# A weight ring of six units in place of four, the low part in the memory of the raw part, stage loops written out

## What is computed

```python
for i in range(DEPTH):
    kind, j = i % N_MIXERS, i // N_MIXERS
    if kind == 0:
        mix = fox_mixer(h, fox_w_in[j], fox_b_f[j], fox_w_o[j])
    elif kind == 1:
        mix = swa_mixer(h, swa_w_in[j], swa_sinks[j], swa_w_o[j], cos_p, sin_p)
    else:
        mix = mla_mixer(h, mla_w_a[j], mla_g_q[j], mla_g_kv[j], mla_w_uq[j], mla_w_ukv[j], mla_w_o[j],
                        cos_m, sin_m)
    h = layer_norm(DEEPNORM_ALPHA * h + mix, ln1_g[i], ln1_b[i])
    ffn = conv_glu_ffn(h, ffn_w_in[i], ffn_conv_w[i], ffn_conv_b[i], ffn_w_out[i], valid)
    h = layer_norm(DEEPNORM_ALPHA * h + ffn, ln2_g[i], ln2_b[i])
```

## Time and profile before

| | |
|---|---|
| median of 3 runs | 1333.57 us (1332.96 to 1334.44) |
| the profiled execution, own time | 1333.88 us |
| its span, first to last instruction | 1332.1 us |
| granted PE clock, mean | 0.995 of full |
| PE busy | 1296.4 us (97%) |
| DVE, ACT, POOL busy | 938.3, 793.8, 225.8 us |
| weights moved | 377 DMAs of 512 KB |

### The profile page before, as it was taken

How to read it: one execution, slowest core, us unless ns; L and a number is a source line. 1 busy time by engine, 2 the same in 40 slices (tenths; PEclk the granted TensorE clock), 3 DMA queues, 4 the chain that set the end, 5 groups by cost and what they waited for, 6 DMA issues and landing times.

```text
span 1332.1 us, 29945 instructions
## 1 busy us (share of the span) xinstructions
PE 1296.4 (97%) x10381; PEld 1252.5 (94%) x10381; DVE 938.3 (70%) x1877; ACT 793.8 (60%) x1625; POOL 225.8 (17%) x208
## 2 busy tenths in 40 slices
PE   7999999999998999999998999999999999999997
PEld 7999999999887999999987899999999899999997
DVE  4765877765787877765678687776567667777665
ACT  4565666654565676664476667666446565766643
POOL 1000044420000034330001003433000000244300
PEclk9999999999999999999998999999999999999999
DMA  7432465556421455556442045555645334465562
GB/s 267 140 110 80 143 189 185 178 180 198 133 91 49 130 185 184 180 155 213 155 127 80 33 143 187 187 172 165 208 139 158 111 112 127 144 187 189 174 218 83
DMA packets 56723, 202.80 MB, mean 152 GB/s; under 512 B 6208, under 2 KB 8256, under 8 KB 56512
## 3 DMA queue, kind: packets, MB, share of 16 engines
q1 hardware_dynamic: 56640, 201.68, 47.4%
HBM read 200.61 MB, written 1.05 MB: 151 GB/s over the span
## 4 chain that ended last, share of the span: by engine, by line
PE 82%; DVE 7%; ACT 5%; issue 3%; DMA 1%; POOL 1%; ACTq 0%; DVEq 0%; POOLq 0%; SPq 0%
PE ps L385 23%; PE ps L389 22%; PE ps L388 22%; PE ps L535 2%; PE ps L553 2%; ACT probs L889 2%; DVE w_lo L1260 1%; PE ps L424 1%; PE ps L518 1%; PE ps L430 1%; PE ps L427 1%; ACT w_hi L839 1%; DMA raw<-in_weights 1%; POOL gated L1234 1%; DVE scores L1320 1%
## 5 line engine op out<-in xcount | busy, mean ns | idle before, releaser
L1260 DVE TENSOR_TENSOR w_lo<-raw,w_hi 128x1024 fp32r<-128x1024 f32 x377 | 461.1, 1225 | 230.3 <-ACT w_hi L839 228.9
L385 PE MATMUL ps<-h_hi,w_hi 128*128 128x272 f32 (+1 forms) x1752 | 508.6, 290 | 1.8 <-DVE q_rope L1526 1.0
L389 PE MATMUL ps<-h_hi,w_lo 128*128 128x272 f32 (+1 forms) x1752 | 505.8, 289 | 0.0
L388 PE MATMUL ps<-h_lo,w_hi 128*128 128x272 f32 (+1 forms) x1752 | 499.6, 285 | 0.0
L839 ACT ACTIVATE w_hi<-raw 128x1024 fp32r<-128x1024 f32 x377 | 395.0, 1050 | 147.7 <-PE ps L385 136.9
L385 PEld LDWEIGHTS ps<-h_hi,w_hi 128*128 128x128 f32 x1752 | 329.1, 188 | 8.4 <-issue 5.4
L388 PEld LDWEIGHTS ps<-h_lo,w_hi 128*128 128x128 f32 x1752 | 330.0, 188 | 0.3
L389 PEld LDWEIGHTS ps<-h_hi,w_lo 128*128 128x128 f32 x1752 | 328.9, 188 | 0.0
L385 PE MATMUL ps<-hid_hi,w_hi 128*128 128x272 f32 (+2 forms) x636 | 185.4, 292 | 2.2 <-DVE w_lo L1260 1.9
L388 PE MATMUL ps<-hid_lo,w_hi 128*128 128x272 f32 (+2 forms) x636 | 183.1, 288 | 0.0
L389 PE MATMUL ps<-hid_hi,w_lo 128*128 128x272 f32 (+2 forms) x636 | 183.0, 288 | 0.0
(11 more groups left out here) (184 smaller groups left out, 1727.3 us busy)
## 6 DMA issues: line engine op xcount, KB each, us to landing
raw<-in_weights SPq DMA_DIRECT2D x377, 512.0 KB, 3.7
cst<-in_consts SPq DMA_DIRECT2D x1, 1795.5 KB, 12.1
h<-in_x SPq DMA_DIRECT2D x2, 544.0 KB, 5.8
out<-h SPq DMA_DIRECT2D x8, 128.0 KB, 1.7
```

The lines of the kernel that those rows point to most:

```text
L385: m = pe.matmul(b, whi, xhi, start=n == 0, stop=False)
L388: pe.matmul(b, whi, xlo, start=False, stop=False)
L389: m = pe.matmul(b, wlo, xhi, start=False, stop=n == len(tiles) - 1)
L1260: return dve.tensor_tensor(out_, a_, b_, op)
```

## The change

The ring has six units instead of four, so `AHEAD` is five instead of three. The total memory stays as it is (twelve buffers of 4 KB a partition): `raw[s]` and `w_lo[s]` now are the same memory, and `split_lo` writes the low part over the raw weights that it reads. A slot therefore comes free for the next DMA only when PE has used its low part, and SP waits for `w_used` instead of `lo_ready`. `turns` writes its turns out instead of looping. SP's own loop stays. The rest of the diff computes the slot from the unit's absolute number.

```diff
-RING = 4
+RING = 6
 ...
-        raw = [sb(f"raw{s}", [P, UNIT]) for s in range(RING)]
+        with ExitStack() as shared:
+            raw = [shared.enter_context(nc.sbuf_tensor(f"raw{s}", [P, UNIT], F32)) for s in range(RING)]
+        w_lo = [sb(f"w_lo{s}", [P, UNIT], F32R) for s in range(RING)]
         w_hi = [sb(f"w_hi{s}", [P, UNIT], F32R) for s in range(RING)]
-        w_lo = [sb(f"w_lo{s}", [P, UNIT], F32R) for s in range(RING)]
 ...
         def turns(eng, n, emit, first=0):
 
-            if n - first == 1:
-                emit(first)
-            elif n > first:
-                with eng.Fori(first, n) as i:
-                    emit(i)
+            for i in range(first, n):
+                emit(i)
 ...
             def unit(u, s):
 
-                sp.wait_ge(lo_ready, u - (RING - 1))
+                sp.wait_ge(w_used, u - (RING - 1))
 ...
-                    slot = (u0 + u) % RING
+                    slot = un % RING
 ...
-                    split_lo(i * s.body_units + first, first % RING)
+                    split_lo(i * s.body_units + first, (i * s.body_units + first) % RING)
```

More of the change, by code:

```diff
@@ L846, in units_of @@
                         continue
-                    yield (i * s.body_units + first, first % RING,
-                           i * (s.body_units // RING) + (first // RING + 1)
-                           if s.turns > 1 else first // RING + 1)
+                    u = i * s.body_units + first
+                    yield u, u % RING, u // RING + 1
             def gemm(layer, name, evac=None, links=0, straight=False):
@@ L1287, in turn @@
                             for u in s.new_units(j)[:-1]:
-                                if i * s.body_units + u0 + u + AHEAD < N_UNITS:
-                                    split_lo(i * s.body_units + u0 + u + AHEAD, (u0 + u + AHEAD) % RING)
+                                coming = i * s.body_units + u0 + u + AHEAD
+                                if coming < N_UNITS:
+                                    split_lo(coming, coming % RING)
                             late()
```

## The result

The changed kernel takes 1470.57 us (median of 4 runs, 1466.75 to 1474.78) against 1333.26 us (4 runs): a ratio of 1.1031 with a 95% interval of 1.0998 to 1.1064. The forecast was 1468. The profiled execution spans 1464.6 us, 132.5 more than before, at a mean clock of 0.957 against 0.995. It is the execution whose own time is 1466.75 us, the fastest of the four.

The account below looks back on a forecast made before the run. PE, busy 1296.4 of 1332.1 us, was taken as the bound, so new waits ahead of it count in full. Stalls of 101.6 us plus 33 us of clock made 134.6 us on 1333.88: 1468 us, range 1425 to 1502.

Parts of the forecast that it names:

- fox pairs: Stages `qk` of two fox layers: scores start 3.03 us later per pair, 7.5 stalls a layer, 45.4 us.
- LayerNorm tails: Ends of `o` and `down`: squares and sums queue behind late splits, 4 x 3.5 + 3 x 3.8 = 25.4 us.
- starts of `up`: Leading panels of four `up` stages: evacuations queue behind a late split, 4 x 2.4 = 9.6 us.
- swa: Sliding stage swa: two stalls of 3.03 us at its first panels, steady part costs 0.
- mla: Stage mla: between one and seven stalls, four taken at 3.03 us, since about half its splits precede an evacuation.
- clock: PE's clock falls behind two in three of 29 new stalls, 1.7 us each: 33 us, ends 0 and 49.
- Trigger to split: A split can't start before 4.15 us after its panel starts: 0.3 matmul, 0.15 issue, 3.7 landing.
- rival D: Faster: landings never hold ACT, and the 1.9 us wait and half clock at last `up` go; 1330 us, chance 0.03.
- A: The stalls come but PE's clock holds: 1435 us, chance 0.13.
- C: Fox stalls half hidden as PE runs on into the other bank: 1436 us, or 1412 with clock held; chance 0.14.
- E: Slots are rebuilt but transfers still run early enough, so no difference; chance 0.03.
- B: Every stall brings a clock fall, and landings take 4.2 instead of 3.7 us: 1499 us, chance 0.17.

Follow-up runs that it names:

- the last experiments: Changed kernel with last splits of `o` and `down` moved behind the LayerNorm: 1453.09 us; `o`'s last split but one too: 1444.45 us; plus fox order turned: 1382.35 us.

## Why the prediction was right, step by step

The path is the forecast one, and the terms can be held against the trace. PE's idle time is what its waits cost; what its busy time has gained with the same 10381 matmuls is the clock (us, both profiled executions):

| Term | forecast | PE idle more | stages longer, clock included |
|---|---|---|---|
| fox pairs | 45.4 | 42.3 | 72.8 |
| LayerNorm tails | 25.4 | 22.1 | 33.1 |
| starts of `up` | 9.6 | 5.3 | 5.5 |
| swa | 6.1 | 5.2 | 7.5 |
| mla | 12.1 | 9.2 | 14.5 |
| start | 3.0 | 2.5 | 3.0 |
| loops, last `down` | 0 | -1.9 | -3.2 |
| all waits | 101.6 | 84.2 | |
| clock | 33 | 48.3 (PE busy more) | |

(The sum of the waits counts in 0.6 us less ahead of the first matmul.) All waits together were taken 17 us too large and the clock 15 us too small. That the sum, 134.6 us, came within 3 us of what was measured (132.5 between the profiled executions, 137.3 between the medians) is luck; the kinds of waits, their places and which of them are the largest are not.

- **Trigger to split, 4.15 us.** Right. Shown in the timeline above (146.30 to 150.45), and by the two runs that put one and two panels between trigger and split. Over the splits that waited, the median from the unit's first matmul to the split is 4.2 us; a quarter of them stand at 4.7 or more, where the transfer itself took 4.2 us or longer. No run shows what makes those longer.
- **Fox pairs, 45.4 us without the clock.** Measured 45.4 us with the clock held, 42.3 us as idle time. That two of these agree to the tenth is luck: six pairs in full and two by half are 7 stalls, not the 7.5 of the sum, which would have been 42.4 us, and 101.3 and 99.6 us still hold short waits behind the put-in matmuls. The size of one stall was right: 12.76 less 9.80 is 2.96 us, where 3.03 was worked out.
- **LayerNorm tails, 25.4 us.** The idle time ahead of line 561 is 3.0 to 3.6 us in each of seven, 22.9 us in all; the kernel before had none there. In full the stages `o` and `down` have 33.1 us more; the rest is mostly the half clock through the sums and the matmuls without use behind them. The working for `o` was near in its sum (3.5 us a stage against 3.0 to 3.4) and incomplete in its picture: it took the last panel's split for the cause, and the chain of sums and joins was late already. Taking the last split away left `o` as long as it was, so the split before it and the chain behind that were just as late.
- **Starts of up, 9.6 us.** Measured 5.5 us: the term is too large by 4. Each `up` has two stalls at the bank (0.6 and 0.7 us in layer 0, 6.1 us in all eight), both within the second turn of four panels, which takes 13.9 us in place of 12.4 in layer 0; from the third turn on the times are within 0.1 us of those of before. So the loss is 1.5 to 1.8 us where I had 2.4.
- **swa's steady part, 0.** Right: its period is the same 7.8 us. The two stalls at its start are there (3.9 and 2.0 us); with the clock swa costs 7.5 us where 6.1 and their clock stood.
- **mla, 12.1 us.** Measured 14.5 with the clock, which fell there once for 13.7 us on end; idle time 9.2. It is one stall of 3.7 us, one of 2.3 and several near 1.0. The count of four stalls was a guess between bounds and no more than that.
- **Start, 3 us.** Measured 3.0, by the cause named (the constants), and gone with their order.
- **The clock, 33 us.** Too small by 15. The mean clock of 0.957 over 1464.6 us means 126 us at half clock, against some 14 us before. I had a fall behind two in three of 29 stalls. In the two `qk` stages each of the 14 stalls at the scores brought one, four of the 16 falls there for 6.8 us in place of 3.4. It isn't a rule without exception: ahead of the LayerNorm sums six of seven stalls brought one, and the idle of 3.42 us that ended at 869.4 did not.
- **Written-out loops, 0.** Right as a sum. In the run with the loops alone, the start of the last `down` gains what rival D said (the prediction put that wait at the end of the last `up`; it stands 10 us into `down`), and the last `up` and `a` give most of it back: from the third on, each turn of four panels of the last `up` takes 11.57 us instead of 11.41, and in `a` the clock falls once for 3.4 us where it did not before. In the changed kernel these turns are back at 11.41 us. What sets the 0.16 us isn't known; no run looked into it.
- **The branch price of the Trainium skill** (Advanced Engine Details and Errata, Control Flow Timing), by the prediction's estimate 4.3 us for 40 turns, doesn't appear: the kernel with the loops alone written out is 0.8 us faster, within its interval of no change.
- **The DMA price of the Trainium skill** (DMA: Bandwidth & Descriptors, Anatomy of one DMA — SWDGE (gpsimd) path), by the prediction's estimate 3.2 us for 512 KB, is for transfers that GpSimd issues. Here SP issues them, and the row after the change says 3.7 us, as the row before did; the sum with 3.7 was the better one.

Of the rivals, A (clock holds, 1435 us) fell with the clock of 0.957 and with the matmuls put in, C with the 41.1 us of idle time at line 510, D with the 4.15 us from trigger to split, E with the result. B is half right: every stall in the fox stages brought a fall, but landings are later only in places.

Two small things in the reading of the rows. Between PE's waits of 2.6 and 2.0 us stand two more, 2.3 us at line 690 and 2.1 us at line 553, which the prediction passed over; no term rests on them. And one of the three half-clock stretches before the change (at 703.17) had a single idle of only 1.07 us close ahead of it, at line 499.

Still open is what holds the `o` stages of the last experiments in detail beyond layer 0; the timeline was read there alone.

## What to carry to other kernels

When a buffer's release and the step that first touches its refill stand at the same point of the program, the full latency of the transfer lands on whatever is queued behind that step, and more depth with the split moved along does not remove it (rings of four and six: 1490 and 1471 us). Leave a distance of at least the landing time between them (here two panels of 3 us for 4.15 us), or put the work that the critical engine waits for ahead of the step that may block. On an engine that is 97% busy, count what stands behind each new wait; the wait itself may be long and free.

## What was not expected

The clock fell at each of the 14 idles ahead of the scores (2.5 to 4.2 us), and 22 matmuls without use in each of 14 gaps made the kernel 21 us faster (1470.57 to 1449.44 us). In layer 0 of the changed kernel the half clock begins between 0.3 us before and 1.5 us after the scores that end a stall. Here the scores start at 139.12 and the half clock lasts from 140.62 to 144.03, through most of the query panel: the matmuls of line 383, every third one, stand 0.68 to 0.70 us apart and then 0.37:

```profile
140.44 0.46 PE L383 MATMUL ps<-h_hi,w_hi 128*128 128x272 f32 x1
141.14 0.43 PE L383 MATMUL ps<-h_hi,w_hi 128*128 128x272 f32 x1
141.82 0.43 PE L383 MATMUL ps<-h_hi,w_hi 128*128 128x272 f32 x1
...
144.32 0.29 PE L383 MATMUL ps<-h_hi,w_hi 128*128 128x272 f32 x1
144.69 0.29 PE L383 MATMUL ps<-h_hi,w_hi 128*128 128x272 f32 x1
```
